# The late tokens' convolution moved into the expert turns, its taps as 32x32 diagonal blocks on TensorE

## The reference

```python
def conformer_conv(h_glu, w_dw, b_dw, ln_g, ln_b, w_pw2, b_pw2):
    a, gate = jnp.split(h_glu, 2, axis=-1)
    h = a * jax.nn.sigmoid(gate)
    h = causal_depthwise_conv(h, w_dw, width=31) + b_dw      # 512 channels
    h = jax.nn.silu(layer_norm(h, ln_g, ln_b))
    return h @ w_pw2 + b_pw2

h = x @ w_in + b_in                       # x: 1024 tokens x 1024
y_conv = conformer_conv(h[:, 0:1024], ...)
y_sb = stick_breaking_attention(q, k, v) @ sb_w_o     # 8 heads of 64, strictly causal
mix = (sigmoid(g_conv) * y_conv + sigmoid(g_sb) * y_sb) @ w_out + b_out
x = layer_norm(alpha * x + mix)
# PEER: per token 8 heads, each picks 16 of 16384 experts by two sets of 128 keys
x = layer_norm(alpha * x + sum over 8 x 16 picked experts of gate * gelu(x . u[idx]) * v[idx])
```

## Time and profile before

| | us |
|---|---|
| three runs | 3177.94, 3178.92, 3179.22 (median 3178.92) |
| the profiled execution | 3178.62 |
| its span, first to last instruction | 3176.8 |
| mean granted PE clock | 0.759 of full speed |
| busy: PE, DVE, ACT, POOL | 2095.0, 2317.0, 1136.7, 1318.6 |
| moved by DMA | 1172.3 MB, 1073.8 MB of them by the gathers |

### The profile page before, as it was taken

The page is one execution under the profiler, slowest core; times in us unless marked ns, Lnnn a source line. Parts: engine busy times, 40 slices in busy tenths (PEclk is TensorE's granted clock), DMA queues, the critical chain, the costliest instruction groups (busy, mean ns, idle before and its releaser), DMA issues.

```text
span 3176.8 us, 53840 instructions
## 1 busy us (share of the span) xinstructions
PE 2095.0 (66%) x20536; PEld 833.8 (26%) x20536; DVE 2317.0 (73%) x4869; ACT 1136.7 (36%) x3349; POOL 1318.6 (42%) x1174
## 2 busy tenths in 40 slices
PE   8899986666788677778987866764343443344333
PEld 7667442222222333333332322220000000000000
DVE  7978577667668999876767866677767777677764
ACT  3234023433324555543433433333333333333332
POOL 0000024444435655543444444444555555555552
PEclk9999998888997877769998888885555555555555
DMA  3111369999999999999999999999999999999996
GB/s 147 53 53 54 134 248 417 420 419 421 419 414 414 420 409 405 411 421 419 420 421 420 418 421 421 419 419 417 420 418 418 420 418 418 418 419 417 418 418 287
DMA packets 167118, 1172.30 MB, mean 369 GB/s; under 512 B 18273, under 2 KB 18401, under 8 KB 30306
## 3 DMA queue, kind: packets, MB, share of 16 engines
q0 software_dynamic: 147456, 1073.81, 81.6%
q1 hardware_dynamic: 19426, 95.26, 7.7%
HBM read 1164.80 MB, written 4.19 MB: 368 GB/s over the span
## 4 chain that ended last, share of the span: by engine, by line
DMA 35%; PE 10%; DVE 7%; issue 6%; ACT 3%; POOL 2%; POOLq 0%; ACTq 0%; DVEq 0%
DMA arena_high<-uv_dram,idx_now 35%; PE ps L906 6%; DVE arena_high L1768 4%; POOL arena_high L671 2%; PE ps L1022 1%; ACT arena_high L1339 1%; ACT wcol L1332 1%; PE ps L832 1%; PE ps L1035 1%; DVE arena_low L1815 1%; ACT gcol L1330 1%; PE ps L981 1%; PE ps L928 0%; DVE arena_low L1818 0%; PE ps L1006 0%
## 5 line engine op out<-in xcount | busy, mean ns | idle before, releaser
L671 POOL DMA_INDIRECT arena_high<-uv_dram,idx_now x1024 | 1253.3, 1224 | 1399.2 <-PE ps L906 1214.2
L1768 DVE SCALAR_TENSOR_TENSOR arena_high<-arena_low,arena_high 128x1024 f32<-128x1024 f32 x1024 | 1245.3, 1224 | 667.8 <-DMA arena_high<-uv_dram,idx_now 661.1
L906 PE MATMUL ps<-arena_high 32*32 32x512 f32 x16384 | 828.7, 845 | 999.6 <-ACT arena_high L1339 998.9
L1330 ACT ACTIVATE gcol<-hcol 128x2 f32<-128x2 f32 x512 | 103.9, 203 | 1614.4 <-DVE arena_high L1768 1613.9
L906 PEld LDWEIGHTS ps<-arena_high 32*32 32x32 f32 x16384 | 136.6, 120 | 1547.2 <-ACT arena_high L1339 1502.2
L1339 ACT ACTIVATE arena_high<-arena_high,wcol 128x32 f32<-128x32 f32 x1024 | 273.1, 314 | 16.7
L1332 ACT ACTIVATE wcol<-gcol,arena_high 128x1 f32<-128x1 f32 x1024 | 245.7, 287 | 16.9
L874 PE MATMUL ps<-arena_low 128*128 128x512 f32 (+1 forms) x512 | 248.7, 627 | 0.0
L666 POOL CAST idx_now<-arena_high 128x8 uint32<-128x8 f32 x128 | 61.9, 483 | 235.1 <-DVE arena_high L1754 234.6
L874 PEld LDWEIGHTS ps<-arena_low 128*128 128x128 f32 x512 | 100.0, 209 | 166.3 <-issue 154.8
L240 PE MATMUL ps<-x_hi_bytes,w_hi_bytes 128*128 128x512 f32 x320 | 129.4, 404 | 13.6 <-DVE x_lo_bytes L1526 8.0
(11 more groups left out here) (176 smaller groups left out, 2498.9 us busy)
## 6 DMA issues: line engine op xcount, KB each, us to landing
arena_low<-slabs_dram SPq DMA_DIRECT2D x20, 1152.0 KB, 10.0
arena_high<-uv_dram,idx_now POOLq DMA_INDIRECT x1024, 12.8
arena_low<-w_mix_dram SPq DMA_DIRECT2D x8, 1536.0 KB, 11.1
arena_high<-w_proj_dram SPq DMA_DIRECT2D x16, 512.0 KB, 3.3
arena_high<-w_mix_dram SPq DMA_DIRECT2D x8, 1024.0 KB, 4.9
arena_high<-xT_dram SPq DMA_DIRECT2D x8, 512.0 KB, 8.6
arena_high<-w_mix_dram SPq DMA_DIRECT2D x8, 512.0 KB, 4.0
arena_high<-w_out_dram SPq DMA_DIRECT2D x2, 2048.0 KB, 10.2
```

The source lines that it names most:

```text
L671: pool.indirect_dma_start(out=ring[:, s % RING, :], out_offset=None, in_=uv_d, in_offset=bass.IndirectOffsetOnAxis(ap=idx_now[:, s:s + 1], ...
L906: last = nc.tensor.matmul(ps[out:out + QUAD, y_bank(t // PH) + turn, :], diag[rows, s % DIAGS, :], ring[rows, s % RING, cs], start=False, ...
L1330: steps.link(nc.scalar.activation(gcol[:, s0:s0 + 2], hcol[:, s0:s0 + 2], ACT.Gelu))
L1768: last = nc.vector.scalar_tensor_tensor(out=ring[:, s % RING, 0:D], in0=x1[c][:, j, :], scalar=1.0, in1=ring[:, s % RING, 0:D], op0=ALU.mu ...
```

## The change

The convolution of the late half leaves the first part altogether. There, PE projects the early half alone (`pe.Fori(0, 4)`, 24 matmuls a job), inputs of the early half alone are loaded, rounded and split, and DVE computes 96 of the 124 early taps before attention and 28 beside its first seven units. The value weights' remainders, two gate splits and the value results' evacuation, which now adds the bias (DVE, no longer ACT, and no bias matmul), stand between taps. Mean and variance of the early half are matmuls in attention units 7 and 10, its centring, reciprocal and scaling follow units 7, 11 and 12 on DVE, its squares, root and swish stand at units 8, 10 and 14 on ACT.

In turns 1 to 8 each channel group c takes two turns. In turn 2c + 1, PE projects gate and value in plain float32 (16 matmuls, steps 1 to 5, banks 7 and 6), ACT makes the gate by tanh at step 4, and DVE at step 6 the product, a copy of the 30 columns that the early half has put by (`pads`), and the tap weights as 31 diagonal 32x32 blocks. In turn 2c + 2, PE computes the 31 taps, each as four matmuls of 32x32 blocks on the diagonal that add up in bank 6 (steps 0 to 5), and ACT adds the bias at step 6. The scores of these turns wait for the banks. Mean, variance and layer norm of the late half move from turns 2 to 4 to turns 9 to 11. On SP two of the eight weight tiles and the late inputs (`xT_part`) are loaded during attention, the other six tiles stand between the slabs 4 to 9.

```diff
-        conv_in_late = at(24, CC, HALF + 2 * (PAD // 2 + 1))
-        conv_in = at(152, 2, HALF + 2 * (PAD // 2 + 1))
...
+        conv_in_late = at(77, HALF + 2 * (PAD // 2 + 1))
+        w_conv = [[at(8 * j + 4 * i, CC, P) for i in range(2)] for j in range(2)]
+        tap_diag = [at(0, TAPS // 2 + 1, QUAD), at(4, TAPS // 2, QUAD)]
+        glu_late = at(8, HALF)
+        pads = [at(204.625, CC - 1, PAD)[:, c, :] for c in range(CC - 1)] + [at(203.3125, PAD)]
...
-                sp_eng.dma_start(xT[:, :, k, :], xT_d[:, k, :, :]).then_inc(xT_in[k], 16)
+                sp_eng.dma_start(xT[:, k, :], xT_d[:, k, 0, :]).then_inc(xT_in[k], 16)
...
                 sp_eng.dma_start(w_branch[:, m % 4, :], w_mix_d[m, :, 2 * D:3 * D]).then_inc(wbranch_in[m % 4], 16)
 
+            def load_conv(c, j):
+
+                if c >= 1 and j == 1:
+                    sp_eng.wait_ge(glu_late_done, c)
+                if c >= 1 and j == 0:
+                    sp_eng.wait_ge(taps_late_done, c)
+                src = w_proj_d[2 * c + j, :, :].rearrange("p (a b) -> p a b", b=HALF)
+                sp_eng.dma_start(kT[:, 2 * j:2 * j + 2, 0:HALF], src).then_inc(wconv_in[j], 16)
+
             sp_eng.wait_ge(proj_done, 4 * CC)
             load_gate(0)
-            sp_eng.wait_ge(var_done, 1)
             load_gate(1)
-            sp_eng.wait_ge(v_done, BLK)
             load_branch(0)
...
                 sp_eng.wait_ge(gates_done, 2 * m - 2)
                 load_gate(m)
+            load_conv(0, 1)
+            load_conv(0, 0)
+            sp_eng.wait_ge(normed, CC)
+            sp_eng.dma_start(xT_part, xT_d[:, :, 1, :]).then_inc(xT_part_in, 16)
...
-            for i in range(4, 7):
-                load_slab(i)
-            sp_eng.wait_ge(normed, 2 * CC)
-            sp_eng.dma_start(xT_part, xT_d[:, :, 1, :]).then_inc(xT_part_in, 16)
-            for i in range(7, LATE_SLAB):
+            for i in range(4, LATE_SLAB):
+                if i - 4 < 2 * (CC - 1):
+                    load_conv((i - 2) // 2, 1 - i % 2)
                 load_slab(i)
...
-            pool.wait_ge(v_done, BLK)
+            pool.wait_ge(v_read, BLK)
             pool.memset(starts[:, P:HALF], 0.0).then_inc(starts_ready, 1)
...
-            with pe.Fori(0, 2) as it:
+            pe.wait_ge(consts, 6)
+
+
+            with pe.Fori(0, 4) as it:
                 for j in range(4):
...
-                        for h in range(2):
-                            last = split_products(ps[:, 2 * j + h, :], (w1_hi_r[:, j, k, :], w1_lo_r[:, j, k, :]),
-                                                  (x_hi_r[:, 1 - h, k, :], x_lo_r[:, 1 - h, k, :]), k == 0, k == KD - 1)
+                        last = split_products(ps[:, 2 * j + 1, :], (w1_hi_r[:, j, k, :], w1_lo_r[:, j, k, :]),
+                                              (x_hi_r[:, k, :], x_lo_r[:, k, :]), k == 0, k == KD - 1)
                     last.then_inc(proj_done, 1)
-            with pe.Fori(2, 4) as it:
...
-            value_block(BLK)
-            pe.wait_ge(conv_done, CC)
-            conv_mean(1, 4)
-            value_block(BLK + 1)
-            value_block(BLK + 2)
-            conv_var(1, 5)
-            value_block(BLK + 3)
-            pe.wait_ge(centred, CC)
-            pe.wait_ge(std_done, 1)
...
+            for b in range(BLK, NB):
+                value_block(b)
...
+                if n == 7:
+                    pe.wait_ge(conv_done, CC)
+                    pe.wait_ge(out_read, 1)
+                    conv_mean(1, 4)
+                if n == 10:
+                    pe.wait_ge(out_read, 2)
+                    conv_var(1, 5)
...
+                if ALONE <= i < LATE_SLAB:
+                    pe.wait_ge(glu_late_done, (i - ALONE) // 2 + 1)
+                if ALONE < i < LATE_SLAB:
+                    pe.wait_ge(conv_late_out, (i - ALONE + 1) // 2)
...
 
             def late_conv_mean():
 
-                pe.wait_ge(conv_done, 2 * CC)
-                pe.wait_ge(score_ready, BLK)
+                pe.wait_ge(conv_late_out, CC)
+                pe.wait_ge(consts, 7)
+                pe.wait_ge(score_ready, LATE_SLAB)
                 conv_mean(0, 6)
+
+            def late_products(c, i):
+
+                k, g = i % KD, i < KD
+                if i == 0:
+                    pe.wait_ge(score_ready, ALONE + 2 * c)
+                if i == 0 and c == 0:
+                    pe.wait_ge(xT_part_in, 16)
+                    pe.wait_ge(x1T_ready, BLK)
+                if k == 0:
+                    pe.wait_ge(wconv_in[int(g)], 16 * (c + 1))
+                last = nc.tensor.matmul(ps[:, 6 + int(g), :], w_conv[int(g)][k // CC][:, k % CC, :], xT_part[:, k, :],
+                                        start=(k == 0), stop=(k == KD - 1))
+                if k == KD - 1:
+                    last.then_inc(conv_g_psum if g else conv_a_psum, 1)
+
+            def late_taps(c, k0, k1):
+
+                if k0 == 0:
+                    pe.wait_ge(score_ready, ALONE + 2 * c + 1)
+                    pe.wait_ge(tap_diag_ready, c + 1)
+                for k in range(k0, k1):
+                    half = k // (TAPS // 2 + 1)
+                    for r in range(P // QUAD):
+                        rows = slice(r * QUAD, (r + 1) * QUAD)
+                        last = nc.tensor.matmul(ps[rows, 6, :], tap_diag[half][rows, k - half * (TAPS // 2 + 1), :],
+                                                conv_in_late[rows, PAD - k:PAD - k + HALF], start=(k == 0),
+                                                stop=(k == TAPS - 1), skip_group_check=True)
+                if k1 == TAPS:
+                    last.then_inc(taps_late_done, 1)
 
             def stick_scores(u, hd):
...
-                if t == 2 and g == 0:
+                c, odd = divmod(t - 1, 2)
+                if 0 <= c < CC and odd == 0 and 1 <= g < 6:
+                    for i in range((0, 0, 3, 6, 9, 12)[g], (0, 3, 6, 9, 12, 16)[g]):
+                        late_products(c, i)
+                if 0 <= c < CC and odd == 1 and g < 6:
+                    late_taps(c, (0, 5, 10, 15, 20, 25)[g], (5, 10, 15, 20, 25, 31)[g])
+                if t == 9 and g == 0:
                     late_conv_mean()
-                if t == 2 and g == 6:
+                if t == 9 and g == 6:
...
+            def late_glu_gate(c):
+
+                act.wait_ge(conv_g_psum, c + 1)
+                b = 2 * KD + c
+                nc.scalar.activation(glu_late, ps[:, 7, :], ACT.Tanh, bias=half_bias[:, b:b + 1],
+                                     scale=0.5).then_inc(glu_tanh, 1)
+                act.wait_ge(glu_tanh, c + 1)
+                nc.scalar.activation(glu_late, glu_late, ACT.Identity, bias=half_col[:, :],
+                                     scale=0.5).then_inc(glu_gate_ready, 1)
+
+            def late_conv_out(c):
+
+                act.wait_ge(taps_late_done, c + 1)
+                nc.scalar.activation(conv_h[0][:, c, :], ps[:, 6, :], ACT.Identity,
+                                     bias=cols[:, C_CB + c:C_CB + c + 1]).then_inc(conv_late_out, 1)
...
-            taps_done = Steps(dve, conv_step)
-            glu(0)
-            for c in range(CC):
-                for k in range(TAPS):
-                    i = c * TAPS + k
-                    if i % 10 == 4 and i // 10 < 12:
-                        split_w1(4 + i // 10)
-                    conv_tap(taps_done, c, 1, k)
-                    if c == 0 and k == TAPS - 1:
-                        glu(1)
-                    if c in (1, 2) and k == TAPS // 2:
-                        glu(c + 1)
-            for k in range(KD):
+                nc.vector.tensor_copy(pads[c], conv_in[:, c, 0:PAD])
...
+            def early_tap(i):
+                c, k = divmod(i, TAPS)
+                conv_tap(taps_done, c, k)
+                if i in (9, 20, 31):
+                    glu((9, 20, 31).index(i) + 1)
+
+            before = CC * TAPS - 28
+            glu(0)
+            for i in range(before):
+                if i % 5 == 2 and i // 5 < 12:
+                    split_w1(4 + i // 5)
+                early_tap(i)
+                if 62 <= i < 78 and i % 2 == 0:
+                    split_values((i - 62) // 2)
+                if i == 82:
+                    split_gates(0)
+                if i == 90:
+                    split_gates(1)
+                if i in (83, 88, 92):
+                    value_out(BLK + (83, 88, 92).index(i))
+            value_out(NB - 1)
...
-                    for i in range(4 * n + 2 * hd, min(4 * n + 2 * hd + 2, 2 * TAPS)):
-                        conv_tap(taps_done, 1 + i // TAPS, 0, i % TAPS)
+                    if n < 7:
+                        for i in range(2):
+                            early_tap(before + 4 * n + 2 * hd + i)
...
+                if n == 7:
+                    conv_centre(1, 4)
+                if n == 11:
+                    conv_rstd(1)
+                if n == 12:
+                    conv_scale(1)
```

(22 more changed lines are left out.)

200 lines of the change are left out of this document (96 added, 104 removed).

## The result

| | before | after |
|---|---|---|
| median us | 3178.43 (4 runs, 3174.27 to 3179.22) | 3156.31 (4 runs, 3154.71 to 3158.36) |
| profiled execution, span | 3178.62, 3176.8 | 3156.83, 3155.0 |
| busy PE, DVE | 2095.0, 2317.0 | 2185.7, 2229.3 |
| moved by DMA | 1172.3 MB | 1174.77 MB |

The ratio is 0.9935, 95% interval 0.9922 to 0.9947: faster by 0.65%, 22 us. The forecast was 3139, its range 3108 to 3184. The direction and the way the change works held; the gain is a little over half of the 39.6 us that were forecast.

A forecast was written before the change was run, and what follows sets the result against it. Hardly anything is loaded in the first part, where DVE's taps are the chain before attention; gathers bound the 64 expert turns. From 3178.6, start -67 and turns +27 gave 3139 us, range 3108 to 3184.

The forecast's parts named there:

- The start: Before the turns: DVE's taps are the chain; scan -73, mean and variance +7, clock -1, in sum -67 us (-58 to -75).
- The tap: Even turns: four overlapping block matmuls on TensorE with covered weight loads take 0.86 us a tap, 26.7 us a turn.
- The bound with uncovered weights: Even turns: two weight loads of 0.104 us left uncovered make a tap 1.07 us, the upper bound.
- rival c: Even turns: few busy blocks get 1.2 GHz, a tap takes 1.72 us, 194 us more, 3333 us; chance 0.12.
- Turns 1 to 8: Expert turns with the added products and taps: TensorE becomes the late one, +27 us in sum, bounds +8 and +58.
- ledger: Turns 1 to 8: TensorE's work summed turn by turn, 363.6 us, against 347.8 us that these turns took before.
- hand-overs: Ends of turns 1 to 8: ACT's score copies and next expert weights leave TensorE waiting 2 us a turn, 16 us.
- credit: After turns 1 to 8: a full ring is worth 0 to 5 gathers of 2.5 us; 5 us taken off.
- main case: Whole kernel: 3139 us, with 3120 to 3156 us; chance 0.55.
- rival (b): Turns 1 to 8: taps or hand-overs cost more, uncovered loads +26 us, giving 3165 us; chance 0.16.
- The transfers: Turns 1 to 8: 1.05 MB more to load, 2.5 us, falls where TensorE sets the pace, inside the 27 us.
- Rival (a): Turns 1 to 8: the ring hides most of TensorE's excess, experts +12 us, giving 3124 us; chance 0.12.

The follow-up runs named there:

- one block: Changed kernel with only one of the four 32x32 blocks computed in each tap but the first and last: 3206.04 us, ratio 1.0082.
- the run with neither products nor taps: Changed kernel without 12 of the 16 products and 29 of the 31 taps of each channel group: 3111.65 us, ratio 0.9793.
- the pairs with 84.7 and 83.5 us of TensorE: Turns 3 and 4 of two edits to the changed kernel: 12 of 16 products left out (3147.01 us); 12 of 31 taps on DVE (3121.07 us).
- the kernel with DVE's taps: Changed kernel with 12 of each group's 31 late taps computed on DVE, 19 left on TensorE: 3121.07 us, again 3122.14 us.

## Why the prediction was right, and where its sum was off

**The start**: forecast -73 for the scan, +7 for mean and variance, -1 for the clock, -67 in sum. Measured -74.0 for the scan and -70.2 at turn 1's first experts. DVE's chain was worked out to 1 us. One statement in it was off and cost nothing: that TensorE waits for DVE by 3 to 5 us before the first scan. It waits while DVE splits the value weights (busy 6.9 of 10.7 us from 96.6 to 107.3). From there to the scan it has no gap (21.60 of 21.60 us), at a clock of 0.94, which the prediction had as a possibility: its last value block ends at 125.3 and it goes on with scores and gates. It waits for DVE only behind the scan, by less than 2 us:

```profile
134.35 0.66 PE L765 MATMUL ps<-arena_high 128*128 128x128 f32 x4 [1.83 <-DVE arena_high L1702]
```

So DVE's chain did set the start, with TensorE ready 2 us before it.

**The tap**: 0.86 to 0.87 us, the value taken. The bound with uncovered weights (1.07) is out: a tap's weight loads (992 records of L1014, median 104 ns) hide completely, and going from eight of them to two with one block left the taps 0.87 us apart at the same clock. In the Trainium skill, "TensorE: Matmul & The Clock Gate", Part 3, says that a weight load overlaps running matmuls only where the row group differs. By that the prediction estimated 26 us more, and the trace disagrees. The same part also lets a load for a background weight buffer go ahead; these taps fit that. In the Trainium skill, "TensorEngine Tiling (Array Packing)", Gotcha 1, says that different row tiles cannot access one PSUM bank at once; here four row groups write one bank, each its own 32 partitions, at the price of one.

**The clock** (rival c): it stood at 1.00 in the even turns, so the 3333 did not come. But the fear had a ground: with one block a tap it fell, and the kernel became slower than before. Of that rival it is right that a chain which keeps few blocks busy can be granted less than the full clock; four blocks and two were granted all of it here, one was not.

**Turns 1 to 8**: this is the term that was mis-sized, 27 us forecast and 49 measured. The prediction had a ledger of 363.6 us, 16 of hand-overs and -5 of credit afterwards, 374.6 against 347.8: +27. Measured, from turn 1 to the end, is +49.3 (-70.2 to -20.9), 22 us more:
- TensorE's work. The ledger's 10 us for closing the block hold 3.1 us of waits (1.81 and 1.32), so 360.5 of it is work. Measured are 376.3 (the eight busy times above), 15.8 more. 7 of it is turn 9's mean and its first four projections, which stand ahead of that turn's first experts and so inside the edges. The rest is spread: a middle step of an even turn is 8.28 us and not 8.0; the clock was 0.94 to 0.97 in the odd turns, for which the ledger had 1.0.
- Idle time, 16 and those 3.1 forecast, measured 399.2 - 376.3 = 22.9: 3.8 more. 8.6 of it are in turn 7 with the closing of the block at its end. The waits themselves are not those named: the three for the slab (2.74 us the longest) were costed at nothing, and the hand-overs are 1.3 and 0.5.
- Credit of the ring, 5 forecast, 2.4 found (from -18.5 at turn 9 to -20.9 at the end).

These three are 15.8 + 3.8 + 2.6 = 22.2. The start was 3.2 better. That gives 19 us; forecast (3139) and profiled execution (3156.83) lie 18 apart.

The 3156 stands at the upper edge of the main case (3120 to 3156), nearer to the 3165 of rival (b) than to 3139. The cause named in (b), uncovered weight loads, is out. That the stated range held owes something to its width: its part for the turns, +8 to +58, had its upper end from those loads, which did not come; the 49 came from the terms above. Two slips in the recorded sums weigh little: no hand-over and the whole credit of 5 gathers give 363.6 - 12.5 - 347.8 = +3, not +8, and an even turn of 51.5 us doubled is 103, not 101.

**The transfers** of 1.05 MB, 2.5 us, were said to be inside the 27. In the run with neither products nor taps they and all else in the turns cost 2.6 us. Whether they cost anything in the changed kernel, where TensorE is the late one, no run tells.

**What the turns cost.** The pair of turns 3 and 4 takes 87.6 us with neither part (40.9 and 46.7 above), by the transfers. Twelve products more in each pair cost 8.8 us over the four pairs, 2.2 for 10.6 us of TensorE's. Above that, TensorE's work is paid nearly in full: 12 taps a turn to DVE are 4 x 10.3 = 41 us off TensorE and 35 off the kernel. Rival (a), that the ring hides most of it, is out: what is saved in one turn does not reach through the next. This is what the pairs with 84.7 and 83.5 us of TensorE show, 95.6 against 89.2. That the reason is the ring's depth, 8 tiles or four steps, is argued; another depth was not tried. Where in turns 7 and 8 the kernel with DVE's taps loses its last us (96.2 for the two, 89.9 with nothing in them) was not taken apart: it is 6.3 of the 10 us by which it still lies above that run.
